# Second attention of the two layers: two sets of tiles for turned steps, and a head's value one round later and in two parts

## The reference, cut to what matters

```python
def mla_attention(...):        # C; B differs in the mask and in the sizes
    ...
    s = jnp.where((kchunk[None, :] <= tc[:, None])[None, None], s, NEG)
    p = jax.nn.softmax(s, axis=-1).astype(v.dtype)
    return jnp.einsum('bhqs,bshd->bqhd', p, v)

x = x + jnp.concatenate([o_a, o_b, o_c], axis=-1) @ w_out
```

## Time and profile before

| | |
|---|---|
| median of three runs | 4076.39 us |
| the profiled execution | 4082.05 us |
| its span, first to last instruction | 4080.2 us |
| TensorE busy | 3840.5 us, 94% of the span, 17196 matmuls |
| VectorE busy | 1940.7 us, 48% |
| ScalarE busy | 1494.4 us, 37% |
| GpSimd (POOL) busy | 381.3 us, 9% |
| granted TensorE clock, mean | 0.967 of full |
| chain that ended last | PE 71%, DVE 8%, ACT 7%, issue 6%, DVEq 5% |

### The profile page before, as it was taken

How to read it: one execution, slowest core, us unless ns; L and a number is a source line. 1 busy time by engine, 2 the same in 40 slices (tenths; PEclk the granted TensorE clock), 3 DMA queues, 4 the chain that set the end, 5 groups by cost and what they waited for, 6 DMA issues and landing times.

```text
span 4080.2 us, 48049 instructions
## 1 busy us (share of the span) xinstructions
PE 3840.5 (94%) x17196; PEld 3036.8 (74%) x17196; DVE 1940.7 (48%) x3222; ACT 1494.4 (37%) x2459; POOL 381.3 (9%) x332
## 2 busy tenths in 40 slices
PE   8999997789999999997799998899999999999999
PEld 6887664678888887564588877787777777777887
DVE  4433457654425433457554334335544444555652
ACT  3222333432223222343432234435544554533221
POOL 0100001101101100001101021011100000100110
PEclk9999998899999999997899999999999999999999
DMA  4333221023333333211033334131112112322332
GB/s 118 95 98 101 80 59 51 10 80 97 94 97 93 98 95 117 59 52 44 14 99 96 108 98 115 44 87 47 47 53 81 47 47 89 87 84 87 98 93 98
DMA packets 484453, 321.98 MB, mean 79 GB/s; under 512 B 10928, under 2 KB 464176, under 8 KB 483280
## 3 DMA queue, kind: packets, MB, share of 16 engines
q1 hardware_dynamic: 479616, 301.81, 25.4%
q0 software_dynamic: 3536, 16.13, 1.2%
q10 hardware_dynamic: 1152, 2.10, 0.1%
HBM read 310.82 MB, written 8.52 MB: 78 GB/s over the span
## 4 chain that ended last, share of the span: by engine, by line
PE 71%; DVE 8%; ACT 7%; issue 6%; DVEq 5%; PEld 1%; DMA 0%; POOLq 0%; ACTq 0%; POOL 0%; PEldq 0%; SPq 0%
PE bank L235 20%; PE bank L237 19%; PE bank L236 19%; ACT w_hi L220 2%; DVE w_lo L227 1%; PE bank L1191 1%; DVEq L2569 1%; PE bank L1202 1%; PE bank L1193 1%; PE bank L1194 1%; PE bank L977 1%; PE bank L1175 1%; PE bank L2207 1%; DVEq L1016 1%; DVEq L2583 1%
## 5 line engine op out<-in xcount | busy, mean ns | idle before, releaser
L235 PE MATMUL bank<-h_hi,w_hi 128*128 128x512 f32 x3064 | 1233.8, 403 | 65.1 <-DVE h_lo L389 24.8
L227 DVE TENSOR_TENSOR w_lo<-w_raw,w_hi 128x1024 fp32r<-128x1024 f32 (+1 forms) x571 | 742.4, 1301 | 1041.0 <-ACT w_hi L220 1037.8
L237 PE MATMUL bank<-h_lo,w_hi 128*128 128x512 f32 x3128 | 1231.4, 394 | 0.0
L236 PE MATMUL bank<-h_hi,w_lo 128*128 128x512 f32 x3064 | 1206.4, 394 | 0.0
L220 ACT ACTIVATE w_hi<-w_raw 128x1024 fp32r<-128x1024 f32 (+1 forms) x571 | 591.5, 1038 | 620.9 <-DMA w_raw<-in_ffn_w_down 315.8
L235 PEld LDWEIGHTS bank<-h_hi,w_hi 128*128 128x128 f32 x3064 | 580.6, 189 | 233.5 <-issue 99.2
L237 PEld LDWEIGHTS bank<-h_lo,w_hi 128*128 128x128 f32 x3128 | 591.8, 189 | 131.3 <-issue 2.5
L236 PEld LDWEIGHTS bank<-h_hi,w_lo 128*128 128x128 f32 x3064 | 581.0, 190 | 115.5 <-issue 2.2
L235 PE MATMUL bank<-g_hi,w_hi 128*128 (+1 forms) x880 | 342.4, 389 | 2.5 <-DVE gu_ring L2585 2.5
L236 PE MATMUL bank<-g_hi,w_lo 128*128 (+1 forms) x880 | 342.3, 389 | 0.0
L237 PE MATMUL bank<-g_lo,w_hi 128*128 (+1 forms) x880 | 342.3, 389 | 0.0
(11 more groups left out here) (456 smaller groups left out, 4602.9 us busy)
## 6 DMA issues: line engine op xcount, KB each, us to landing
w_raw<-in_w_in SPq DMA_DIRECT2D x105, 512.0 KB, 3.8
w_raw<-in_ffn_w_gate SPq DMA_DIRECT2D x88, 512.0 KB, 3.8
w_raw<-in_ffn_w_up SPq DMA_DIRECT2D x88, 512.0 KB, 3.8
w_raw<-in_ffn_w_down SPq DMA_DIRECT2D x88, 512.0 KB, 3.5
w_raw<-in_w_mix SPq DMA_DIRECT2D x50, 512.0 KB, 4.0
w_raw<-in_w_up SPq DMA_DIRECT2D x44, 512.0 KB, 3.8
w_raw<-in_w_branch SPq DMA_DIRECT2D x32, 512.0 KB, 3.8
w_raw<-in_w_down SPq DMA_DIRECT2D x22, 512.0 KB, 3.3
```

The lines of the kernel that those rows point to most:

```text
L227: dve.tensor_tensor(WL[:, slot(c), 0:w], RAW[:, slot(c), 0:w], WH[:, slot(c), 0:w].bitcast(F32), ALU.subtract).then_inc(w_lo, 1)
L235: pe.matmul(bank, wh, xh, start=start, stop=False)
L236: pe.matmul(bank, wl, xh, start=False, stop=False)
L237: return pe.matmul(bank, wh, xl, start=False, stop=stop)
```

## The change

The tiles for turned steps of the second attention hold two heads. Heads with an even number lie right of the diagonal of a 4 x 5 grid of 128-wide blocks, the others left of it, mirrored; the transposes of the odd heads therefore go to mirrored places in their bank (`place`). The high tile stays where it was, the low tile moves to 94 KB of the work area. The value product of head h is issued one round later: its three 512-wide matmuls (key tile 0) in round 4h+8 and the other nine in round 4h+9, after Q·K of the round and before its transposes, as before. ScalarE's first copy of a head waits for the value of the head before the last one instead of the last one. The y of a pair is copied and split two rounds later, in round 8p+13. One round is added at the end of each stage. Nothing changes in the list of matmuls, copies, subtractions and DMAs but their order and places.

```diff
--- before.py
+++ after.py
@@ -588,7 +588,8 @@
     def turned_pair(name, hi_at, lo_at):
         return (sb(name + "_hi", [P, TURNED], F32R, hi_at), sb(name + "_lo", [P, TURNED], F32R, lo_at))
 
-    PT_CB = turned_pair("cb_turned", G0 + 52 * KB, G0 + 52 * KB + 6656)
+    ROW = 5 * P
+    PT_CB = (g("cb_turned_hi", 52, [P, 24 * P], F32R), sb("cb_turned_lo", [P, 24 * P], F32R, G0 + 94 * KB))
     PT_X = turned_pair("turned", X_AT, X_AT + 6656)
     WI = sb("index_weights", [P, TT, 8])
     M8 = sb("eight_largest", [P, 8])
@@ -1104,26 +1105,47 @@
 
     class Places:
 
-        def __init__(self, scores, turned, n_turned, probs, parts=None, late=False):
+        def __init__(self, scores, turned, n_turned, probs, parts=None, late=False, two_sets=False):
+            self.two_sets = two_sets
+            self.values_at = [((0,), (1, 2, 3))[k] for k in range(2)] if two_sets else [range(TT)]
+            self.delay = len(self.values_at) - 1
             self.scores, self.turned, self.n_turned, self.probs, self.parts = scores, turned, n_turned, probs, parts
             self.late = late
             self.copied, self.subtracted, self.used = (TT, TT + 1, 2 * TT + 1) if late else (LAG, LAG, 2 * TT - 1)
+            if two_sets:
+                self.used = 2 * TT
             self.rounds = self.used - TT + 2
 
-        def block(self, part, x):
-
-            tile = self.parts[part]
-            at = x["i"] * P
-            return tile[:, at:at + (x["i"] + 1) * KEY_STRIDE].rearrange("p (k c) -> p k c", c=KEY_STRIDE)[:, :, 0:P]
-
-        def keys(self, part, kt):
-
-            return self.parts[part][:, kt * KEY_STRIDE + kt * P:kt * KEY_STRIDE + S]
+        def block(self, part, x, h):
+
+            tile, i = self.parts[part], x["i"]
+            if not self.two_sets:
+                at, stride = i * P, KEY_STRIDE
+            elif h % 2 == 0:
+                at, stride = (i + 1) * P, ROW
+            else:
+                at, stride = (TT - 1 - i) * ROW, ROW + P
+            return tile[:, at:at + (i + 1) * stride].rearrange("p (k c) -> p k c", c=stride)[:, :, 0:P]
+
+        def keys(self, part, kt, h):
+
+            if not self.two_sets:
+                at = kt * KEY_STRIDE + kt * P
+            elif h % 2 == 0:
+                at = kt * ROW + (kt + 1) * P
+            else:
+                at = (TT - 1 - kt) * ROW
+            return self.parts[part][:, at:at + S - kt * P]
+
+        def place(self, m, kt):
+
+            return m % TT - kt if self.two_sets and m // TT % 2 else kt
 
     WITH_PROJECTIONS = Places(lambda n, w: B[n % 2][:, 0:w], lambda m, a, b: B[2 + 2 * (m % 2)][:, a:b], 2,
                               lambda m, w: (GU[:, 0, 0:w], GU[:, 1, 0:w], PROB2[:, 0:w], PROB3[:, 0:w])[m % 4], PT_X)
     IN_CB = Places(lambda n, w: B[n % 2][:, 0:w], lambda m, a, b: B[(2, 3, 6)[m % 3]][:, a:b], 3,
-                   lambda m, w: (SG[:, 0, 0:w], SG[:, 1, 0:w], TMP[:, 0:w], T[:, 0, 0:w])[m % 4], PT_CB)
+                   lambda m, w: (SG[:, 0, 0:w], SG[:, 1, 0:w], TMP[:, 0:w], T[:, 0, 0:w])[m % 4], PT_CB,
+                   two_sets=True)
 
     def split_act(act, jobs, j, s0, waits=()):
 
@@ -1178,28 +1200,32 @@
                 if x["extra"]:
                     last = pe.matmul(bank, *x["extra"], start=False, stop=True)
                 last.then_inc(qk_done, 1)
-            if n >= at.used and (n - at.used) % TT == 0 and n - at.used < len(steps):
-                h = (n - at.used) // TT
+            h, part = (n - at.used) // TT, (n - at.used) % TT
+            if n >= at.used and part < len(at.values_at) and h * TT < len(steps):
                 x = steps[h * TT]
-                if h % 2 == 0:
-                    pe.wait_ge(sp_lo, s0 + (3 * (h // 2) + 3))
-                    pe.wait_ge(y_lo, y0 + (h // 2 + 3 - banks))
-                pe.wait_ge(pl_done, l0 + (TT * h + TT + 2))
+                if part == 0:
+                    if h % 2 == 0:
+                        pe.wait_ge(sp_lo, s0 + (3 * (h // 2) + 3))
+                        pe.wait_ge(y_lo, y0 + (h // 2 + 3 - banks))
+                    pe.wait_ge(pl_done, l0 + (TT * h + TT + 2))
                 cols = slice(64 * x["half"], 64 * x["half"] + P)
-                for kt in range(TT):
+                for kt in at.values_at[part]:
                     out_ = B[x["bank"]][:, kt * P:S]
-                    pe.matmul(out_, VH[:, kt, cols], at.keys(0, kt), start=(h % 2 == 0 and kt == 0), stop=False,
+                    pe.matmul(out_, VH[:, kt, cols], at.keys(0, kt, h), start=(h % 2 == 0 and kt == 0), stop=False,
                               skip_group_check=True)
-                    pe.matmul(out_, VLO[:, kt, cols], at.keys(0, kt), start=False, stop=False, skip_group_check=True)
-                    last = pe.matmul(out_, VH[:, kt, cols], at.keys(1, kt), start=False,
+                    pe.matmul(out_, VLO[:, kt, cols], at.keys(0, kt, h), start=False, stop=False,
+                              skip_group_check=True)
+                    last = pe.matmul(out_, VH[:, kt, cols], at.keys(1, kt, h), start=False,
                                      stop=(h % 2 == 1 and kt == TT - 1), skip_group_check=True)
-                last.then_inc(hv_done, 1)
+                if part == at.delay:
+                    last.then_inc(hv_done, 1)
             if LAG <= n < len(steps) + LAG:
                 m = n - LAG
                 pe.wait_ge(nrm_done, n0 + (m + 1))
                 pe.wait_ge(pl_done, l0 + (m + 3 - at.n_turned))
                 for kt in range(m % TT + 1):
-                    last = pe.transpose(at.turned(m, kt * P, (kt + 1) * P), at.probs(m, S)[:, kt * P:(kt + 1) * P],
+                    to = at.place(m, kt)
+                    last = pe.transpose(at.turned(m, to * P, (to + 1) * P), at.probs(m, S)[:, kt * P:(kt + 1) * P],
                                         c_block(C_ID))
                 last.then_inc(tr_done, 1)
             yield
@@ -1220,10 +1246,10 @@
                 w = steps[m]["width"]
                 act.wait_ge(tr_done, n0 + (m + 3))
                 if m % TT == 0:
-                    act.wait_ge(hv_done, h0 + (m // TT + 1))
-                act.activation(at.block(0, steps[m]), at.turned(m, 0, w).rearrange("p (k c) -> p k c", c=P), ACT.Copy
+                    act.wait_ge(hv_done, h0 + (m // TT + (0 if at.two_sets else 1)))
+                act.activation(at.block(0, steps[m], m // TT), at.turned(m, 0, w).rearrange("p (k c) -> p k c", c=P), ACT.Copy
                                ).then_inc(pt_done, 1)
-            pair = pair_taken(n - TT - at.used, len(steps))
+            pair = pair_taken(n - TT - at.used - at.delay, len(steps))
             if pair is not None:
                 act.wait_ge(hv_done, h0 + (2 * pair + 3))
                 for bank, dst_hi, dst_lo in y_of(steps[8 * pair]["group"]):
@@ -1246,8 +1272,8 @@
             for m in turned_at(n - at.subtracted, len(steps), at.late) if at.late else ():
                 w = steps[m]["width"]
                 dve.wait_ge(pt_done, n0 + (m + 3))
-                dve.tensor_tensor(at.block(1, steps[m]), at.turned(m, 0, w).rearrange("p (k c) -> p k c", c=P),
-                                  at.block(0, steps[m]).bitcast(F32), ALU.subtract).then_inc(pl_done, 1)
+                dve.tensor_tensor(at.block(1, steps[m], m // TT), at.turned(m, 0, w).rearrange("p (k c) -> p k c", c=P),
+                                  at.block(0, steps[m], m // TT).bitcast(F32), ALU.subtract).then_inc(pl_done, 1)
             if n < len(steps):
                 x = steps[n]
                 if hook:
@@ -1270,9 +1296,9 @@
             for m in turned_at(n - at.subtracted, len(steps), at.late) if not at.late else ():
                 w = steps[m]["width"]
                 dve.wait_ge(pt_done, n0 + (m + 3))
-                dve.tensor_tensor(at.block(1, steps[m]), at.turned(m, 0, w).rearrange("p (k c) -> p k c", c=P),
-                                  at.block(0, steps[m]).bitcast(F32), ALU.subtract).then_inc(pl_done, 1)
-            pair = pair_taken(n - TT - at.used - (1 if at.late else 0), len(steps))
+                dve.tensor_tensor(at.block(1, steps[m], m // TT), at.turned(m, 0, w).rearrange("p (k c) -> p k c", c=P),
+                                  at.block(0, steps[m], m // TT).bitcast(F32), ALU.subtract).then_inc(pl_done, 1)
+            pair = pair_taken(n - TT - at.used - at.delay - (1 if at.late else 0), len(steps))
             if pair is not None:
                 for bank, dst_hi, dst_lo in y_of(steps[8 * pair]["group"]):
                     dve.wait_ge(y_hi, y0 + (pair + 1))
```

## The result

| | before | changed |
|---|---|---|
| median, 20 runs each in turn on one chip | 4075.46 us (4069.67 to 4084.06) | 4084.92 us (4074.59 to 4091.83) |
| ratio, 95% interval | | 1.0020 (1.0013 to 1.0027) |
| span of the profiled execution | 4080.2 us | 4083.0 us |

The change costs 0.2%, 5 to 11 us. The forecast was a gain of 3.7 us. The time lies inside the stated range, but the kernel got slower where it was forecast to get faster.

A forecast was written before the change was run, and what follows sets the result against it. No engine was full; VectorE's loop with ScalarE was the one to follow. Gains at other heads less lost cover and low clock gave +2.5 and +1.2 us per layer, 3.7 together: median 4072.7 us, own range 4068 to 4081, wider range 4056 to 4089.

The forecast's parts named there:

- What bounds it, and what the change removes: Second attention: VectorE's loop with ScalarE is to be followed; idle time after a value goes, at most 24.3 us.
- The lost cover: Pair starts, rounds 16, 24, 32: Q·K meets POOL's wait without the value before it; 3.4, 1.9, 0.3 us lost, first layer.
- The term for the clock: Round 24: 1.0 us lost at full clock, some 2 us more at half clock for value, Q·K and transposes.
- the middle: Round 24: a loss between the full-clock and half-clock cases, 1.9 us in each layer.
- Head 8 to 9: Distance between the last two heads' markers: idle time of 2.86 and 2.94 us falls to 0.47; 2.4 and 2.5 gained.
- The tail: End of each stage: only the last head is left to wait, 0.6 us gained per layer.
- C: Rival, pair starts and next heads: TensorE at 1.2 GHz becomes the bound; 16.5 us lost, 4092.9 us; chance 0.18.
- The prediction's own sign for it: Marker distances: 11 us and more at the even heads would mean C.
- A: Rival, pair starts: POOL is done before TensorE arrives and the whole idle time goes; 4052.1 us; chance 0.10.
- B: Rival: clock stays up after the 2.3 us gaps, round 16 loses half; 10.9 us gained, 4065.5 us; chance 0.17.
- D: Rival, whole kernel: the waits change place only and nothing is gained; 4076.4 us; chance 0.05.
- The rule weighed: Eight pair starts: VectorE and POOL share a port pair; one more hit each costs 5.6 us, forecast 4078; none taken.

The follow-up runs named there:

- ninth experiment: The changed kernel plus unused matmuls: eight ahead of Q·K's wait for POOL, five ahead of the value's wait for odd heads and head 8; 4058.98 us, ratio 0.9971.
- seventh experiment: The kernel before plus five unused 512-wide matmuls ahead of each value's wait for the low part; 4062.93 us, ratio 0.9965.
- fourth experiment: The changed kernel plus eight unused 512-wide matmuls ahead of Q·K's wait for POOL at rounds 8, 16, 24 and 32; 4068.59 us, ratio 0.9984.
- first experiment: The kernel before with only the change's tile layout, the value staying whole in round 4h+7; 4077.08 us, ratio 1.0003.
- fifth experiment: The changed kernel with an even head's value issued whole ahead of Q·K in round 8p+8, odd heads unchanged; 4061.82 us, ratio 0.9966.
- tenth experiment: The changed kernel with even heads' values whole ahead of Q·K, plus five unused matmuls ahead of each value's wait; 4049.08 us, ratio 0.9944.
- second experiment: The changed kernel with the high parts of the next pair's Q and K made four rounds earlier; 4065.82 us, ratio 0.9976.

## Why the prediction was wrong

**What bounds it, and what the change removes: right.** VectorE's loop is the bound where the clock is up: 9.1 us per head were forecast, and heads 4 to 5 and 6 to 7 took 9.12 and 9.32 in the first layer. The value's wait (7.8 us, forecast under 8), the idle time before the 128-wide low part (0.47 us) and Q·K's new waits for POOL came as forecast.

**The lost cover: right in place, and right in size at round 24 with the clock up.** The wait for POOL came at rounds 16, 24 and 32, 4.64, 2.40 and 2.19 us long. Set against each other with the gaps filled (ninth and seventh experiment, first layer), head 5 to 6 takes 10.88 against 9.99 (0.9 lost, forecast 1.0 with the clock up) and head 7 to 8 8.06 against 8.33. At round 16 the forecast distance was 15.2 us; 13.82 and 14.66 came, so the loss there was put too high (3.4 and 3.9 for 2.1 and 3.3). Part of that is a slip in the sum: 3.3 + 5.3 + 3.3 puts the maximum of round 18 at +11.9 and not at +12.2. For round 32 the 7.7 us at full clock doesn't follow from its terms either, since 10.8 - 2.3 is 8.5, or 8.35 with POOL's end at +0.65 instead of +0.8; 8.07 was measured.

**The term for the clock: too small, and this is the step that failed.** At round 24 the prediction had a loss of 1.0 us for a clock that stays up, "some 2 us more" for one that doesn't, and took the middle, 1.9. At round 32 it had 7.7 us for the distance with the clock up and 10.1 with it down, and took a loss of 0.3 on 8.39. Measured losses: 4.1 and 3.9 at round 24, 2.5 and 2.6 at round 32. In all four places the clock went down, so the middle was the wrong place to stand. And where it is down the loss is 3.0 us on top (13.90 - 10.90, the fourth experiment), not 2: everything that is queued behind the gap runs at half speed ahead of the transposes that VectorE waits for at 776.82. The middle at round 24 leaned on one row in which the clock stayed up, after 1.40 us, against one of 1.86 in which it didn't, though the new gap was put at 2.3 us, longer than both.

The rule cited from the Trainium skill, "TensorE: Matmul & The Clock Gate", section "Why this matters for your kernels" (keep idle gaps short), is borne out in kind: the clock fell behind the gap of 2.40 us at POOL's wait. By that rule alone the prediction had fewer long gaps at the value as a gain; its reading of the rows, that the gap moves and doesn't go, is what the trace shows, but it priced the moved gap too low.

**Head 8 to 9: wrong for the same reason.** The 2.4 and 2.5 us were to come from the idle time before the 128-wide low part. It did go (2.86 us at 811.25 before), but after round 32 the clock stays low until 810 us, and the 2.56 us at 810.26 took its place. With the gaps filled the new order has 10.20 us there (ninth experiment) and the old one 11.63 (seventh), so the gain is there once the clock is up.

**Luck and smaller misses.** The second layer's head 2 to 3 and 4 to 5 lost 0.7 and 0.9 us instead of giving 1.6 and 0.5: a gap of 1.40 us before 1938.97, at the value, was followed by a clock of 0.56 and then 0.50 to 1946, and one of 1.06 us before 1966.14 by 0.50 from 1968 to 1970. The first layer's head 4 to 5, forecast +2.5 and measured +3.6, is in the main luck: the 12.71 us of the base belong to one execution, and the first experiment had 9.74 there in the old order. The tail gave 1.9 and 2.1 us for 0.6: the last low part of y came 9.78 and 9.66 us behind its marker, for 11.66 and 11.79. That gain, undersized by 2.8 us in both layers together, hides part of the loss.

**The sum.** The stages take 250.3 us before and 239.1 with the gaps filled, 258.0 changed and 235.8 filled. Filling gives back 11.2 us of the old order and 22.2 us of the new one; the difference, 11.0 us, turns a loss of 7.7 us into a lead of 3.3. By the ratios filling gives back 14 and 20 us, a difference of only 6 us, which is no more than the width of the intervals, and filled the new order is 2.4 us behind the old one (0.9971 and 0.9965, with intervals that overlap). So the two orders can't be told apart once their gaps are filled, and that 3.3 us lies near the forecast's 3.7 confirms nothing.

**The rivals.** C named the mechanism: the low clock after each gap of 2.3 us, for 6 us. It had 16.5 us lost, measured 8. The prediction's own sign for it, distances of 11 us and more at the even heads, came at head 8 to 9 in both layers (12.97 and 12.98) and at head 2 to 3 in the second (12.00), not at 4 to 5 and 6 to 7. In the first layer it had the pairs' starts nearly right (heads 3, 5 and 7 to the next: 3.8, 3.2 and 1.8 lost, measured 2.1, 4.1 and 2.5), but charged the heads behind them too much (4 to 5 and 6 to 7: 1.3 gained and 1.5 lost, measured 3.6 and 0.6 gained). A was refuted by the wait for POOL: with the cover given back, by the fifth experiment, the gain is 14 us, and it takes the filled gaps as well (tenth experiment, 23 us) to come near the 24 that A had. B needed a clock that stays up, and it didn't at rounds 24 and 32. D, no change, is just outside the interval. The rule weighed, that POOL and VectorE get in each other's way, would have added hits on VectorE. No term needs them: VectorE's low parts of turned steps kept a mean of 491 ns and ScalarE's copies 422 ns in both kernels. VectorE's normalising in the first layer had a mean of 426 ns before and 434 ns after.

Open: why the clock went down after 0.57 us of idle time in one place (778.39, second experiment) and stayed up after 0.57 and 2.49 us in others (781.94 in the changed kernel; 1966.36 before), and why it stayed down for 16 us behind round 32 and for six behind round 24.

## What to carry to other kernels

Before a move that takes the cover from a wait, look at what TensorE's clock does behind gaps of that length in the same trace, and price the gap with everything that queues up behind it at half speed; where the rows show both outcomes, take them as two cases, not as their mean. Look at more than one execution before a term is read from one distance: one of 12.71 us was 9.74 in another trace of the same order. A wait on another engine that can't be avoided is best met with real work in front of it (here an even head's value: 22 us less than the change); where there is none, even unused matmuls paid (14 and 15 us). Compare two orders with the clock up on both sides before one is thrown away: this one was 8 us worse as it stood, and with the gaps of both filled the two couldn't be told apart.

## What the runs showed of the hardware

TensorE's clock fell from 2.4 to 1.2 GHz behind single idle gaps as short as 0.57 us (778.39, second experiment), 1.40 us (757.15, the same) and 2.40 us (769.39, the change). Other gaps of 0.57 us (781.94, the change) and 2.49 us (1966.36, before) left it up, and a gap of 1.41 us did the one in one execution and the other in another. Once down it stayed down for six us behind 769.39 and for 16 us behind 793, though TensorE was busy without a break. Filling gaps with matmuls that nothing reads, 64 in the changed kernel and 100 in the one before, took 15 and 14 us off, though eight of them keep TensorE busy for 2.09 us.
